# State powers ahead of the third weighed block, and four modulation parts in 32-row strips, in the setup of a two-block transformer kernel

## The chip, the cores and the metric

One core of one Trainium2 chip. The metric is the device time of one execution in microseconds (us), as the median of several runs. Engines: PE is TensorE (matmul), DVE is VectorE, ACT is ScalarE, POOL is GpSimd, SP is SyncE, which here only issues DMAs.

## What is computed

The reference is two transformer blocks, one after the other, in float32 over x of 1024 positions by 1024 channels. The change touches only the start of the first block:

```python
mod = (c @ w_ada + b_ada)[:, None, :]             # c: (1, 1024), w_ada: (1024, 6144)
sh_m, sc_m, gt_m, sh_f, sc_f, gt_f = jnp.split(mod, 6, axis=-1)
h = rms_norm(x, g_pre_mix) * (1.0 + sc_m) + sh_m
z = h @ w_in                                      # (1024, 1280)
u, f, q, k, v = jnp.split(z, splits, axis=-1)
y_ssm = s5_mixer(u, lam_re, lam_im, log_dt, b_re, b_im, c_re, c_im, d_skip, w_glu)
y_fft = fourier_mixer(f, w_fft)
y_att = window_attention(q, k, v, sink)
```

The state-space mixer runs h[t] = lam_bar h[t-1] + b_bar u[t] in both directions for 24 groups of 64 complex states. The kernel does it in chunks of 8 positions, so it needs lam_bar^k b_bar and lam_bar^k c for k up to 8, and lam_bar^(8 * 2^m) to carry states over chunks.

## The kernel before

The order of the work is written out by hand: each engine has one list of instructions, and semaphores join them. All that follows lies in the first 8% of the span.

**The modulation row** c @ w_ada has 12 parts of 512 columns. The first four (0 and 1 are the shift, 2 and 3 the scale) are needed for h. `FIRST_ORDER` is (0, 2, 1, 3). For each, `modulation(j)` on PE (L4239 to L4247) runs eight float32 matmuls. Their stationary operand is a column of c broadcast to 128 columns (`c_bcast`, L3872), so that all 128 rows of a PSUM bank hold the same sums, and `modulation_used(j)` on DVE (L4013 to L4034) picks the diagonal with four multiply-and-reduce instructions against the identity, and adds the bias. The other eight parts are weighed by `weigh_block(b)` on DVE (L4036 to L4052): eight pieces of 128 by 512, each loaded by SP into one of four buffers (`load_block`, L3705), times a column of c, added up in `ada_acc`; `sum_block(b)` on PE sums it over the partitions with four matmuls by a column of ones.

**The loop over x.** ACT squares x (L3777), and DVE and ACT scale half of its rows each (L3863, L3785). In the loop over eight k (L4356 to L4361), PE transposes the columns of x for k + 1 (`turn_input`), ACT applies shift and scale to each half (L3815: one pass for the first half, two for the second), DVE splits off the rounded part (`split_input`, L4116 and L4118), and PE runs `unit_step(0, k)`, six matmuls of unit 0 of h @ w_in. ACT waits for `mod_ready` 1 ahead of the first half (parts 0 and 2) and `mod_ready` 2 ahead of half 8 (parts 1 and 3). Nine more units follow from L4363 on, PE on its own but for `split(n)`: ACT rounds the weights of unit n (L3796) once unit n - 2 is done, and DVE takes the rest (L4109). `sum_block`, `filters` (L4314, 48 matmuls in strips of 32 output rows) and `turn_state` stand in between.

**The state powers.** `lam_step(k)` (L4084 to L4098, six DVE instructions) makes lam_bar^k b_bar for k = 1 to 7. Step 7 releases `lam_b_ready`, for which `filters` waits, and POOL: its `carry_step` chain (L4198) stops there after the first five of its sixteen steps. `square` (L4131 to L4141), nine times, makes the chunk powers `pw`. DVE ends the stage with `weigh_block(7)`, `fold_fourier` (L598 to L602), `late_modulations` (L4054), a wait for `carry_ready` 2 from POOL's last step, and `turns(v, steps, 0)` (L575 to L590), which reads `pw`. Then it copies the transposes of u (L610), for which PE waits at L317; behind them PE runs the chunk transposes, the DFT (14 us) and the attention.

**On DVE**, from the end of the loop over x, the order is: lam 1, split 2, weigh 0, lam 2, split 3, weigh 1, lam 3, split 4, weigh 2, lam 4, split 5, weigh 3, lam 5, split 6, lam 6, the nine squares, lam 7, split 7, weigh 4, first taps, split 8, weigh 5, last taps, weigh 6, split 9, weigh 7.

Of the kernel before, what the change touches and what calls it, by code (L numbers as in the profile page):

```python
# [27 lines left out]
CH = 8  # L28
# [33 lines left out]
def body(ctx, nc, a, out):  # L62
# [49 lines left out]
    junk = place("junk", [P, D], GR + 32 * KB)  # L112
    junk2 = place("junk2", [P, P], RR + 39 * KB + 256)
    c_plain = place("c_plain", [P, 2, PAIRS, GC], RR + 37 * KB)
# [3 lines left out]
    mod_sum = place("mod_sum", [P, 4, KD], RR + 39 * KB)  # L118
    c_bcast = place("c_bcast", [P, KD, P], RR + 40 * KB)
    b_rows = place("b_rows", [4 * PAIRS, P * GC], GR + 40 * KB)  # L120
# [39 lines left out]
    b_turned, lam_used = lam_turned, dt_spread  # L160
    taps_copied, TAPS_0 = dt_spread, 3
    prm_angle, prm_trig, prm_lam = (sem(n) for n in ("prm_angle", "prm_trig", "prm_lam"))
# [3574 lines left out]
    def _(act):  # L3737
# [33 lines left out]


        act.wait_ge(x_in, 16 * NT)
        for n in range(NT):
# [31 lines left out]
        for i in range(2 * KD):  # L3806
            k = i // 2
            act.wait_ge(x_turned, i + 1)
            if i >= 2:
                act.wait_ge(h_ready, i - 1)  # L3810
            if i == KD:
                act.wait_ge(mod_ready, 2)
            half = slice(HALF * (i % 2), HALF * (i % 2 + 1))
            for dst in (h_tmp[i % 2][:], x_hi[:, k, half])[0:1 + i % 2]:
                ins = nc.scalar.activation(dst, bank(6 + i % 2), ACT.Identity, scale=mod_cols[:, 1, k:k + 1], bias=mod_cols[:, 0, k:k + 1])  # L3815
            ins.then_inc(h_made, 1)
            if i == 1:
# [49 lines left out]
    def _(dve):  # L3867
# [3 lines left out]
        dve.wait_ge(small_in, 16)  # L3871
        v.tensor_copy(c_bcast[:], c_cols[:].unsqueeze(2).to_broadcast([P, KD, P])).then_inc(c_spread, 1)  # L3872
        dve.wait_ge(ssm_in, 16 * 4)
# [139 lines left out]
        def modulation_used(j):  # L4013

            dve.wait_ge(ada_mm, FIRST_ORDER.index(j) + 1)
            part, half = j // 2, j % 2
            ps = bank(FIRST_BANKS[j])
            for k in range(4):
                kk = 4 * half + k
                dst = stat_c[:, kk:kk + 1] if part else mod_cols[:, 0, kk:kk + 1]  # L4020

                ins = v.tensor_tensor_reduce(junk2[:], ps[:, P * k:P * (k + 1)], ident[:], 1.0, 0.0, ALU.mult, ALU.add, dst)
                if k < 3:
                    steps.add(ins)
                    steps.settle()
            ins.then_inc(ada_used, 1)
            dve.wait_ge(ada_used, FIRST_ORDER.index(j) + 1)
            cols = slice(4 * half, 4 * half + 4)
            sums = stat_c[:, cols] if part else mod_cols[:, 0, cols]
            steps.add(v.tensor_tensor(sums, sums, bias_cols[:, part, cols], ALU.add))  # L4030
            steps.settle()
            if part:
                steps.add(v.scalar_tensor_tensor(mod_cols[:, 1, cols], sums, 1.0, norm_cols[:, 0, cols], ALU.add, ALU.mult))
                steps.settle()  # L4034
# [138 lines left out]
        weigh_block(4)  # L4173
        first_taps()
        split(8)
# [55 lines left out]
    def _(pe):  # L4231
        t = nc.tensor
        wide = 2 * D_FF // P

        def modulation(j):

            if j == 0:
                pe.wait_ge(ada_half, 16 * KD // 2)
            else:  # L4239
                pe.wait_ge(ada_block[j], 16 * KD)  # L4240
            for k in range(KD):
                if j == 0 and k == KD // 2:
                    pe.wait_ge(ada_block[j], 16 * KD // 2)
                elif j == 3 and k == 5:
                    turn_input(0)
                ins = t.matmul(bank(FIRST_BANKS[j]), c_bcast[:, k, :], ada_w[j][:, k, :], start=(k == 0), stop=(k == KD - 1))
            ins.then_inc(ada_mm, 1)  # L4247
# [15 lines left out]
        def sum_block(b):  # L4263
# [4 lines left out]
            ins.then_inc(ada_mm, 1)  # L4268

        def spread_row(i):  # L4270

# [16 lines left out]
        ins.then_inc(lam_turned, 1)  # L4288
        pe.wait_ge(c_spread, 2)
        modulation(0)  # L4290
        pe.wait_ge(dt_spread, 3)
# [13 lines left out]
        modulation(2)  # L4305
        pe.wait_ge(vec_in, 16 * 8)
# [4 lines left out]
                    ident[0:2 * wide + 4 * KD, 0:2 * wide + 4 * KD]).then_inc(rows_turned, 1)  # L4311
        for j in FIRST_ORDER[2:]:
            modulation(j)

# [37 lines left out]


        pe.wait_ge(ada_used, 2)
        pe.wait_ge(win_lo, 1)
        for k in range(KD):  # L4356
            if k + 1 < KD:
                turn_input(k + 1)
            pe.wait_ge(h_ready, 2 * k + 2)
            ins = unit_step(0, k)  # L4360
        ins.then_inc(win_mm, 1)  # L4361
        for n in range(1, len(win_units)):
# [3 lines left out]
            for k in range(KD):  # L4366
                if 3 <= n <= 6 and k == 1:
                    sum_block(n - 3)
                elif n == 6 and k == 3:
                    filters()  # L4370
                elif n == 6 and k == 7:
                    turn_filters()
                elif n == 7 and k == 4:
                    pe.wait_ge(taps_copied, TAPS_0 + 4)
                    sum_block(4)
                elif n == 8 and k in (1, 6):
                    sum_block(5 + k // 6)
                elif n == 9 and k == 3:
                    sum_block(7)
                if n == 7 and k >= 4:  # L4380
# [58 lines left out]
```

## Time and profile before

| | |
|---|---|
| median of 3 runs | 2896.89 us (2896.32 to 2898.9) |
| the profiled execution's own time | 2893.79 us |
| its span | 2892.0 us |
| PE busy in the span | 2781.0 us (96%) |
| DVE busy | 2066.2 us (71%) |
| ACT busy | 1338.2 us (46%) |
| POOL busy | 247.0 us (9%) |
| granted clock of PE, mean | 0.989 |

The span is the stretch of the trace; 1.8 us of the execution's time lie around it. Times in rows count from the start of the span. A granted clock of 1.00 is 2.4 GHz, 0.50 is 1.2 GHz. A row of a timeline gives start, length, engine and line, and in brackets how long the engine stood idle before it and what released it. Lengths of PE rows are modelled and overlap the next row a little; the difference of two starts is the safer measure.

### The profile page before, as it was taken

Reading aid. Unit: us, or ns where it says so; the run is one execution under the profiler, and the core shown is the slowest. Engines: PE = TensorE matmul, PEld = TensorE weight load, DVE = VectorE, ACT = ScalarE, POOL = GpSimd, SP = SyncE. Lnnn points to the kernel's source line nnn. Section 1 sums busy time; section 2 is a strip of 40 time slices with the busy share of each in tenths; the row PEclk is TensorE's granted clock in tenths of the full one; section 3 lists DMA queues with packets and bytes.
Section 4 is the critical chain, followed back from the end, with each engine's and each line's share of the span. In section 5 each row is a group of like instructions: output and inputs, shape, how many; then the busy total and the mean of one; then the engine's idle time right before and its main releaser. Section 6 shows DMA issues by size and latency. Waiting matters only on the chain.

```text
span 2892.0 us, 37335 instructions
## 1 busy us (share of the span) xinstructions
PE 2781.0 (96%) x13579; PEld 2223.7 (77%) x13579; DVE 2066.2 (71%) x3689; ACT 1338.2 (46%) x2352; POOL 247.0 (9%) x282
## 2 busy tenths in 40 slices
PE   7998899999999999999999999998999999999997
PEld 4874677788888888888888886785677888888886
DVE  6877438989898568766666676897838866665568
ACT  4224746544444554433333453677744433333443
POOL 2063200000000000000000000223610000000000
PEclk9999999999999999999999999999999999999998
DMA  7551043344446773445447763111033355446854
GB/s 236 159 165 23 10 145 124 118 159 155 154 161 230 265 252 120 145 154 168 161 152 281 244 194 110 39 42 34 2 115 111 131 167 164 153 153 211 295 192 145
DMA packets 345429, 436.83 MB, mean 151 GB/s; under 512 B 29701, under 2 KB 191533, under 8 KB 345070
## 3 DMA queue, kind: packets, MB, share of 16 engines
q1 hardware_dynamic: 342290, 428.46, 45.3%
q10 hardware_dynamic: 2956, 5.99, 0.6%
q8 instruction: 108, 1.77, 0.3%
q14 instruction: 75, 0.61, 0.1%
HBM read 317.59 MB, written 116.50 MB: 150 GB/s over the span
## 4 chain that ended last, share of the span: by engine, by line
PE 72%; DVE 7%; ACT 2%; POOL 1%; issue 1%; DMA 0%; DVEq 0%; SPq 0%; ACTq 0%
PE psum L2011 39%; PE psum L1462 21%; PE psum L2974 4%; PE psum L2002 3%; PE psum L1102 2%; DVE count_junk L3505 1%; PE psum L3177 1%; PE psum L3190 1%; PE psum L3164 1%; PE psum L3054 0%; ACT sign_junk L3271 0%; DVE x_t L1708 0%; DVE x_b L2481 0%; POOL p L3672 0%; POOL p_wide L3672 0%
## 5 line engine op out<-in xcount | busy, mean ns | idle before, releaser
L1462 PE MATMUL psum<-far_op,far_op 128*128 128x512 f32 x2772 | 629.4, 389 | 0.0
L1462 PEld LDWEIGHTS psum<-far_op,far_op 128*128 128x128 f32 x2772 | 520.1, 188 | 108.0
L2011 PE MATMUL psum<-x_b,w_near 128*128 128x512 f32 x1440 | 346.0, 389 | 0.8 <-DVE w_near L1634 0.8
L2011 PE MATMUL psum<-x_t,w_near 128*128 128x512 f32 x1440 | 336.5, 389 | 1.7 <-ACT psum L1748 1.7
L2011 PE MATMUL psum<-x_t,w_far 128*128 128x512 f32 x1440 | 336.3, 389 | 0.0
L2011 PEld LDWEIGHTS psum<-x_t,w_near 128*128 128x128 f32 x1440 | 270.2, 188 | 58.2 <-ACT psum L1748 2.1
L2011 PEld LDWEIGHTS psum<-x_b,w_near 128*128 128x128 f32 x1440 | 270.2, 188 | 57.3 <-issue 1.2
L2011 PEld LDWEIGHTS psum<-x_t,w_far 128*128 128x128 f32 x1440 | 270.2, 188 | 56.3 <-ACT u_keep L1760 0.2
L1226 ACT CAST far_op<-far_a 128x512 fp32r<-128x512 f32 x231 | 143.9, 623 | 315.9 <-PE psum L1462 305.4
L1233 DVE TENSOR_TENSOR far_op<-far_a,far_op 128x512 fp32r<-128x512 f32 x231 | 159.8, 692 | 176.4 <-ACT far_op L1226 175.1
L2011 PE MATMUL psum<-x_b,w_far 128*128 128x512 f32 x720 | 173.1, 389 | 1.7 <-DVE val_row L1880 1.7
L3640 POOL TENSOR_TENSOR split_lo<-raw,split_hi 128x256 fp32r<-128x256 f32 (+1 forms) x60 | 44.8, 781 | 1458.3 <-ACT split_hi L2990 1458.3
L1235 DVE TENSOR_TENSOR far_op<-far_b,far_op 128x512 fp32r<-128x512 f32 x231 | 159.2, 689 | 0.0
L1634 DVE TENSOR_TENSOR w_far<-w_sum,w_far 128x512 fp32r<-128x512 f32 x120 | 82.4, 686 | 106.4 <-ACT w_far L1628 106.4
L2011 PEld LDWEIGHTS psum<-x_b,w_far 128*128 128x128 f32 x720 | 135.1, 188 | 30.1 <-DVE val_row L1880 2.1
L1227 ACT CAST far_op<-far_b 128x512 fp32r<-128x512 f32 x231 | 142.1, 615 | 0.0
L1628 ACT CAST w_far<-w_sum 128x512 fp32r<-128x512 f32 x120 | 73.9, 616 | 119.0 <-PE psum L2011 119.0
L1634 DVE TENSOR_TENSOR w_near<-w_sum,w_near 128x512 fp32r<-128x512 f32 x120 | 80.9, 688 | 64.1 <-ACT w_near L1628 64.0
L1628 ACT CAST w_near<-raw 128x512 fp32r<-128x512 f32 (+1 forms) x129 | 82.8, 642 | 72.3 <-PE psum L2011 61.3
L1634 DVE TENSOR_TENSOR w_far<-raw,w_far 128x512 fp32r<-128x512 f32 (+1 forms) x66 | 47.2, 715 | 88.6 <-ACT w_far L1628 88.6
L1079 DVE TENSOR_TENSOR src_lo<-yc_t,src_hi 128x512 fp32r<-128x512 f32 x31 | 21.4, 692 | 119.0 <-ACT w_out_hi L1072 119.0
L2002 PE MATMUL psum<-x_b,w_near 128*128 128x512 f32 x360 | 90.8, 400 | 8.5 <-DVE x_b L2319 4.1
(531 smaller groups left out, 4769.7 us busy)
## 6 DMA issues: line engine op xcount, KB each, us to landing
far_a<-row_ops SPq DMA_DIRECT2D x231, 256.0 KB, 3.0
row_ops<-hidden SPq DMA_DIRECT2D x99, 512.0 KB, 5.6
raw<-in_ffn_w SPq DMA_DIRECT2D x88, 512.0 KB, 4.7
col_sums<-hidden SPq DMA_DIRECT2D x66, 512.0 KB, 5.7
far_b<-col_sums SPq DMA_DIRECT2D x132, 256.0 KB, 3.5
raw<-in_w_up SPq DMA_DIRECT2D x44, 512.0 KB, 3.9
hidden<-in_ffn_w SPq DMA_DIRECT2D x44, 512.0 KB, 5.2
far_b<-in_ffn_w SPq DMA_DIRECT2D x66, 256.0 KB, 3.6
```

The costliest lines, as they stand in the source:

```text
L1102: ins = t.matmul(bank(2 * n + c), l[:, P * n:P * (n + 1)], r[:, HALF * c:HALF * (c + 1)], start=(first and m == 0), stop=(last and m == 2))
L1226: s.copy(far_a_hi[slot][:], far_a[late][t % FB][:]).then_inc(f_hi, 1)
L1227: s.copy(far_b_hi[slot][:], far_b[late][t % FB][:]).then_inc(f_hi, 1)
L1233: v.tensor_tensor(far_a_lo[slot][:], far_a[late][t % FB][:], far_a_hi[slot][:], ALU.subtract).then_inc(f_lo, 1)
L1235: v.tensor_tensor(far_b_lo[slot][:], far_b[late][t % FB][:], far_b_hi[slot][:], ALU.subtract).then_inc(f_lo, 1)
L1462: ins = t.matmul(bank(b + n), l[slot][:, rows], r[slot][:], start=(fresh and i == 0 and m == 0), stop=(i == FH - 1 and m == 2), skip_group ...
L1628: nc.scalar.copy(op_parts(p, i)[0], op_source(p, i)).then_inc(op_hi, 1)
L1634: nc.vector.tensor_tensor(lower, op_source(p, i), upper, ALU.subtract).then_inc(op_lo, 1)
L2002: ins = t.matmul(bank(b), at[:, l, cols], r, start=(first and m == 0), stop=(last and m == 2))
L2011: ins = t.matmul(bank(b), at[:, l, cols], x[:, k, r], start=(start and k == 0 and m == 0), stop=(k == 3 and m == 2), skip_group_check=not ...
L2974: ins = t.matmul(bank(2 * slot + half)[0:m], l[:, P * k:P * k + m], r[:, k, HALF * half:HALF * (half + 1)], start=(k == 0 and i == 0), sto ...
L3640: ins = g.tensor_tensor(tile_of(w_rest, m)[:, k:k + 2], tile_of(raw[slot], m)[:, k:k + 2], tile_of(w_top, m)[:, k:k + 2], ALU.subtract)
```

## The change

`c_bcast` becomes `c_strip`, 32 columns for each k, and each of the first four parts is made in two steps: `strips(j)`, eight matmuls of which number k writes the 32 rows of strip k % 4 of the bank, and `strip_sums(j)`, four matmuls that take a copy of the bank as the stationary operand and a column with a one in each strip (`sel_cols`) as the moving one, so that the part comes out as columns. ACT makes the copy (`copy_strips`). `modulation_used` is left with the bias and the scale. Parts 1 and 3 move into the loop over x. On DVE the powers 3 to 7 are made in a row before the third weighed block, and the squares go behind the last one.

```diff
+        def copy_strips(j):
+            at = FIRST_ORDER.index(j)
+            act.wait_ge(strips_done, STRIPS_0 + at + 1)
+            act.wait_ge(dt_spread, 3)
+            if at:
+                act.wait_ge(ada_mm, at)
+            nc.scalar.copy(ada_part[:], bank(FIRST_BANKS[j])).then_inc(mod_copied, 1)
+
+        copy_strips(0)
         act.wait_ge(x_in, 16 * NT)
...
         nc.scalar.activation(stat_b[:, 0:NT], stat_a[:, NT:2 * NT], ACT.Sqrt).then_inc(x_std, 1)
+        copy_strips(2)
...
             if i == 1:
                 split(1)
+            elif i in (3, 5):
+                copy_strips(i - 2)
...
-            if n == 7:
+            if n == 6:
                 act.wait_ge(k_mm, 1)
...
-            for k in range(4):
-                kk = 4 * half + k
-                dst = stat_c[:, kk:kk + 1] if part else mod_cols[:, 0, kk:kk + 1]
-                ins = v.tensor_tensor_reduce(junk2[:], ps[:, P * k:P * (k + 1)], ident[:], 1.0, 0.0, ALU.mult, ALU.add, dst)
...
-            steps.add(v.tensor_tensor(sums, sums, bias_cols[:, part, cols], ALU.add))
+            steps.add(v.tensor_tensor(sums, bank(FIRST_BANKS[j], 4), bias_cols[:, part, cols], ALU.add))
...
             split_input(i)
-            if i == 2:
+            if i == 4:
+                split(1)
+            elif i == 5:
                 modulation_used(1)
-            elif i == 4:
+            elif i == 7:
                 modulation_used(3)
                 dve.sem_inc(mod_ready, 1)
-            elif i == 7:
-                split(1)
...
         lam_step(1)
-        for b in range(4):
-            split(2 + b)
-            weigh_block(b)
-            lam_step(2 + b)
+        split(2)
+        weigh_block(0)
+        lam_step(2)
+        split(3)
+        weigh_block(1)
+        lam_step(3)
+        lam_step(4)
+        split(4)
+        for k in range(5, CH):
+            lam_step(k)
+        split(5)
+        weigh_block(2)
         split(6)
-        lam_step(CH - 2)
-        square(pw[:, 0, 1], pw[:, 1, 1], col(12), col(10))
-        for src, dst in ((1, 2), (2, 0)) + tuple((m, m + 1) for m in range(6)):
-            square(pw[:, 0, dst], pw[:, 1, dst], pw[:, 0, src], pw[:, 1, src], pw[:, :, src])
-        lam_step(CH - 1)
+        weigh_block(3)
+        first_taps()
         split(7)
         weigh_block(4)
-        first_taps()
...
         dve.sem_inc(fw_zero, 1)
+        square(pw[:, 0, 1], pw[:, 1, 1], col(12), col(10))
+        for src, dst in ((1, 2), (2, 0)) + tuple((m, m + 1) for m in range(6)):
+            square(pw[:, 0, dst], pw[:, 1, dst], pw[:, 0, src], pw[:, 1, src], pw[:, :, src])
         fold_fourier(dve, v, steps)
...
+                s = k % 4
+                ins = t.matmul(bank(FIRST_BANKS[j])[32 * s:32 * (s + 1)], c_strip[:, k, :], ada_w[j][:, k, :], start=(k < 4), stop=(k >= 4))
+            ins.then_inc(strips_done, 1)
+
+        def strip_sums(j):
+            pe.wait_ge(mod_copied, COPIED_0 + FIRST_ORDER.index(j) + 1)
+            for i in range(4):
+                ins = t.matmul(bank(FIRST_BANKS[j], 1, i), ada_part[:, P * i:P * (i + 1)], sel_cols[:], start=True, stop=True)
             ins.then_inc(ada_mm, 1)
...
+        SUMS_AT = ((3, 1), (4, 1), (6, 1), (7, 1), (7, 6), (8, 2), (8, 7), (9, 4))
...
+        turn_input(0)
         pe.wait_ge(ada_used, 2)
         pe.wait_ge(win_lo, 1)
         for k in range(KD):
             if k + 1 < KD:
                 turn_input(k + 1)
+            if k in (1, 2):
+                strips(2 * k - 1)
+            if k in (2, 3):
+                strip_sums(2 * k - 3)
             pe.wait_ge(h_ready, 2 * k + 2)
             ins = unit_step(0, k)
```

On PE, `strips(0)` with its sums stands behind the transposes of b and c, and `strips(2)` with its sums behind those of the vectors; `modulation(1)` and `modulation(3)`, which stood between them and the first transposes of x, are gone. `filters` moves from step (6, 3) of the units to (5, 2), `turn_filters` from (6, 7) to (5, 6), and `sum_block(b)` goes by `SUMS_AT`: before, it stood at k = 1 of units 3 to 6, then at (7, 4), (8, 1), (8, 6) and (9, 3).

## Rows read from the trace of the kernel before

**Rows 1.** The page, first line.
```profile
span 2892.0 us, 37335 instructions
```

**Rows 2.** Windows: stretch, length, busy us of PE, PEld, DVE, ACT, POOL, PEclk, DMA share, GB/s.
```profile
24.00:26.00 2.00, 0.00 (x0) 0.00 (x0) 1.85 (x6) 0.00 (x0) 0.00 (x0) 0.50 1.04 402
...
34.00:36.00 2.00, 2.00 (x4) 0.87 (x3) 1.97 (x5) 1.94 (x5) 1.82 (x4) 0.50 1.05 385
...
38.00:40.00 2.00, 2.00 (x6) 0.80 (x6) 0.00 (x0) 1.97 (x3) 1.92 (x5) 1.00 0.96 355
...
78.30:151.20 72.90, 72.90 (x424) 60.85 (x423) 60.88 (x115) 13.48 (x16) 10.96 (x13) 1.00 0.60 176
...
151.20:192.76 41.56, 41.56 (x226) 35.16 (x224) 29.82 (x39) 11.89 (x17) 40.30 (x52) 1.00 0.55 163
```

**Rows 3.** Timeline of PE, setup: start us, us, engine, line, what [idle before <-releaser].
```profile
31.38 10.05 PE L4246 MATMUL psum<-ada_w,c_bcast 128*128 128x512 f32 x16 [8.67 <-DMA ada_w<-in_w_ada]
...
41.47 11.33 PE L4246 MATMUL psum<-ada_w,c_bcast 128*128 128x512 f32 x26
...
56.88 0.71 PE L4349 MATMUL psum<-x_hi,win_upper 128*128 128x512 f32 x2
...
60.88 0.73 PE L4349 MATMUL psum<-x_hi,win_upper 128*128 128x512 f32 x2 [1.33 <-DVE x_lo L4118]
...
69.45 0.73 PE L4349 MATMUL psum<-x_hi,win_upper 128*128 128x512 f32 x2
...
76.81 0.73 PE L4349 MATMUL psum<-x_hi,win_upper 128*128 128x512 f32 x2 [0.68 <-DVE x_lo L4118]
```

**Rows 4.** Timeline of ACT, setup.
```profile
49.41 1.03 ACT L3796 CAST win_upper<-win_raw 128x1024 fp32r<-128x1024 f32 x1
...
53.34 1.45 ACT L3815 ACTIVATE h_tmp<-psum,mod_cols 128x512 f32<-128x512 f32 x2 [2.90 <-PE psum L4260]
```

**Rows 5.** Timeline of DVE, setup.
```profile
45.29 2.74 DVE L3863 TENSOR_SCALAR x_rows<-x_rows,stat_b 128x1024 f32<-128x1024 f32 x4
...
51.38 1.22 DVE L4109 TENSOR_TENSOR win_lower<-win_raw,win_upper 128x1024 fp32r<-128x1024 f32 x1 [0.22 <-DVE mod_cols L4033]
...
54.61 0.69 DVE L4118 TENSOR_TENSOR x_lo<-h_tmp,x_hi 128x512 fp32r<-128x512 f32 x1
```

**Rows 6.** Timeline of PE and ACT: the nearest rows for the new operations.
```profile
140.69 2.83 PE L4322 MATMUL psum<-lam_b,c_pad 128*32 128x128 f32 x96
...
156.50 0.94 PE L4267 MATMUL psum<-one_cols,ada_acc 128*128 128x1 f32 x8
...
157.98 0.59 ACT L3790 COPY state_in<-psum 128x512 f32<-128x512 f32 x1 [4.76 <-PE psum L4341]
```

**Rows 7.** Lines of DVE from 80 to 140, then 140 to 182: busy us, mean ns.
```profile
L4049 DVE SCALAR_TENSOR_TENSOR ada_acc<-ada_piece,c_cols,ada_acc 128x512 f32<-128x512 f32 x28 | 21.0, 751 | 7.3 <-DMA ada_piece<-in_w_ada 5.2
...
L4049 DVE SCALAR_TENSOR_TENSOR ada_acc<-ada_piece,c_cols,ada_acc 128x512 f32<-128x512 f32 x28 | 24.0, 855 | 6.9 <-DMA ada_piece<-in_w_ada 4.8
```

**Rows 8.** Timeline of DVE, later.
```profile
131.62 0.18 DVE L4134 TENSOR_TENSOR prm<-prm 128x24 f32<-128x24 f32 x1
...
136.69 0.56 DVE L4090 TENSOR_TENSOR w_tmp<-lam_b,prm 128x384 f32<-128x384 f32 x1
...
152.35 1.22 DVE L4109 TENSOR_TENSOR win_lower<-win_raw,win_upper 128x1024 fp32r<-128x1024 f32 x1 [0.28 <-ACT win_upper L3796]
...
180.85 1.11 DVE L4049 SCALAR_TENSOR_TENSOR ada_acc<-ada_piece,c_cols,ada_acc 128x512 f32<-128x512 f32 x1 [0.49 <-DMA ada_piece<-in_w_ada]
...
182.61 0.95 DVE L598 TENSOR_TENSOR f_diff<-f_t 128x511 f32<-128x511 f32 x1
...
194.23 0.07 DVE L575 MEMSET turn<- 128x12 f32 x1 [5.50 <-POOLq L4227]
```

**Rows 9.** Timeline of POOL, then of PE.
```profile
139.93 1.53 POOL L4208 TENSOR_TENSOR e_tmp<-carry_out,prm 128x192 f32<-128x192 f32 x1 [95.42 <-DVEq L4097]
...
208.32 3.53 PE L317 MATMUL psum<-ident,u_t 128*128 128x128 f32 x16 [5.69 <-DVE u_rows L610]
```

More of the change, by code:

```diff
@@ L112, in body @@
     junk = place("junk", [P, D], GR + 32 * KB)
-    junk2 = place("junk2", [P, P], RR + 39 * KB + 256)
+    sel_cols = place("sel_cols", [P, 1], RR + 39 * KB + 256)
+    ada_part = place("ada_part", [P, HALF], RR + 40 * KB)
     c_plain = place("c_plain", [P, 2, PAIRS, GC], RR + 37 * KB)
@@ L118, in body @@
     mod_sum = place("mod_sum", [P, 4, KD], RR + 39 * KB)
-    c_bcast = place("c_bcast", [P, KD, P], RR + 40 * KB)
+    c_strip = place("c_strip", [P, KD, P // 4], RR + 43 * KB)
     b_rows = place("b_rows", [4 * PAIRS, P * GC], GR + 40 * KB)
@@ L160, in body @@
     b_turned, lam_used = lam_turned, dt_spread
-    taps_copied, TAPS_0 = dt_spread, 3
+    mod_copied, COPIED_0, strips_done, STRIPS_0 = dt_spread, 3, c_turned, 2
+    taps_copied, TAPS_0 = dt_spread, 7
     prm_angle, prm_trig, prm_lam = (sem(n) for n in ("prm_angle", "prm_trig", "prm_lam"))
@@ L3871, in _ @@
         dve.wait_ge(small_in, 16)
-        v.tensor_copy(c_bcast[:], c_cols[:].unsqueeze(2).to_broadcast([P, KD, P])).then_inc(c_spread, 1)
+        steps.add(v.memset(sel_cols[:], 0.0))
+        steps.settle()
+        for s in range(4):
+            steps.add(v.memset(sel_cols[32 * s:32 * s + 1], 1.0))
+        steps.add(v.tensor_copy(c_strip[:], c_cols[:].unsqueeze(2).to_broadcast([P, KD, P // 4])))
+        steps.settle()
+        dve.sem_inc(c_spread, 1)
         dve.wait_ge(ssm_in, 16 * 4)
@@ L4015, in modulation_used @@
             dve.wait_ge(ada_mm, FIRST_ORDER.index(j) + 1)
-            part, half = j // 2, j % 2
-            ps = bank(FIRST_BANKS[j])
-            for k in range(4):
-                kk = 4 * half + k
-                dst = stat_c[:, kk:kk + 1] if part else mod_cols[:, 0, kk:kk + 1]
-                ins = v.tensor_tensor_reduce(junk2[:], ps[:, P * k:P * (k + 1)], ident[:], 1.0, 0.0, ALU.mult, ALU.add, dst)
[L4023 to L4028, printed above, removed]
+            part, cols = j // 2, slice(4 * (j % 2), 4 * (j % 2) + 4)
             sums = stat_c[:, cols] if part else mod_cols[:, 0, cols]
-            steps.add(v.tensor_tensor(sums, sums, bias_cols[:, part, cols], ALU.add))
+            steps.add(v.tensor_tensor(sums, bank(FIRST_BANKS[j], 4), bias_cols[:, part, cols], ALU.add))
             steps.settle()
+            dve.sem_inc(ada_used, 1)
             if part:
@@ L4233, in _, with strips @@
         wide = 2 * D_FF // P
[L4235 to L4240, printed above, removed]
+        def strips(j):
+            pe.wait_ge(ada_half if j == 0 else ada_block[j], 16 * KD // (2 if j == 0 else 1))
             for k in range(KD):
@@ L4243, in modulation @@
                     pe.wait_ge(ada_block[j], 16 * KD // 2)
-                elif j == 3 and k == 5:
-                    turn_input(0)
-                ins = t.matmul(bank(FIRST_BANKS[j]), c_bcast[:, k, :], ada_w[j][:, k, :], start=(k == 0), stop=(k == KD - 1))
+                s = k % 4
[5 more added lines that the diff above has]
+                ins = t.matmul(bank(FIRST_BANKS[j], 1, i), ada_part[:, P * i:P * (i + 1)], sel_cols[:], start=True, stop=True)
             ins.then_inc(ada_mm, 1)
@@ L4288, in _ @@
         ins.then_inc(lam_turned, 1)
-        pe.wait_ge(c_spread, 2)
-        modulation(0)
         pe.wait_ge(dt_spread, 3)
@@ L4304, in _ @@
             ins.then_inc(c_turned, 1)
-        modulation(2)
+        pe.wait_ge(c_spread, 2)
+        strips(0)
+        strip_sums(0)
         pe.wait_ge(vec_in, 16 * 8)
@@ L4311, in _ @@
                     ident[0:2 * wide + 4 * KD, 0:2 * wide + 4 * KD]).then_inc(rows_turned, 1)
-        for j in FIRST_ORDER[2:]:
-            modulation(j)
+        strips(2)
+        strip_sums(2)
         def filters():
@@ L4366, in _ @@
             for k in range(KD):
-                if 3 <= n <= 6 and k == 1:
-                    sum_block(n - 3)
-                elif n == 6 and k == 3:
+                if (n, k) == (5, 2):
                     filters()
-                elif n == 6 and k == 7:
+                elif (n, k) == (5, 6):
                     turn_filters()
[L4373 to L4379, printed above, removed]
+                elif (n, k) in SUMS_AT:
+                    if (n, k) == SUMS_AT[2]:
+                        pe.wait_ge(taps_copied, TAPS_0 + 4)
+                    sum_block(SUMS_AT.index((n, k)))
                 if n == 7 and k >= 4:
```

## The prediction

> **What bounds the kernel now.** I read the page first, then the windows and timelines of the first 210 us, since the change touches nothing later. The span is 2892.0 us [rows 1], so what is at stake is 8% of it. The windows show one long stretch in which PE never stops: 72.90 of 72.90 us from 78.30 to 151.20, 41.56 of 41.56 from there to 192.76 [rows 2]. Those are units 1 to 9 with their sums, filters and transposes. Here DVE, ACT and POOL cost nothing as long as they are in time, and the stretch moves with the end of unit 0. Two places are not bound so. Ahead of it, the first matmul of unit 0 starts at 56.88 and unit 0 ends at 78.30, that is 21.4 us for what the even steps 4 to 7, 2.45 us each (69.45 to 76.81), would do in 19.6; PE idles, 1.33 us ahead of step 1 alone [rows 3]. Behind it, PE stands idle 5.69 us until 208.32 for the copies of u [rows 9], which wait on DVE behind `turns`, and `turns` stood idle 5.50 us until 194.23 for POOL's last step [rows 8]. So the time is set by three pieces: the start of the loop, the loop, and DVE's tail behind the last weighed block.
>
> **Start of the loop.** Before, PE was in parts 2, 1 and 3 nearly all the time from 31.38 to the loop (10.05 us for the first of them, at a clock of 0.50 in part, then 26 instructions in 11.33) [rows 2, 3]. Each part becomes strips. The nearest row is `filters`: 96 instructions of 128 columns in strips of 32 rows in 2.83 us, 29.5 ns each [rows 6], where the full-width rows give 11.33 / 26 = 436 ns for 512 columns [rows 3], or 109 for 128: the strips run nearly four at a time. So 16 instructions take 16 x 436 x 29.5 / 109 = 1.9 us instead of 7.0, at full clock. From both sides: 7.0 if they don't overlap at 512 columns, 1.75 if they overlap fully. I take 1.9, for `filters` has the same order of strips in one bank. The sums are like `sum_block`, 0.94 of which 0.8 is its own; the copy is 0.59, like that of `state_in` [rows 6].
> DVE has its x rows scaled at 45.29 + 2.74 = 48.0. The two parts cost it 3.3 us until 51.38 [rows 5]; now three small instructions, some 0.7. What is late next is ACT, which ends scaling at 49.41 and rounds unit 0's weights until 50.44 [rows 4]. So `split(0)` on DVE starts at 50.5, not 51.38, and ACT's first half at 50.5, not 53.34, where it had waited 2.90 for PE's transposes [rows 4]. After 1.22 for the split and 1.1 + 0.6 for the halves (cast 0.43 and a subtraction of 0.69 [rows 5]) both halves are there at 53.4. **Unit 0 starts at 53.5, 3.4 us earlier.** Strips 0 and 2, their sums, and copies on ACT stand in PE's and ACT's waits for DMA and cost nothing; if that cover were gone, strips 2, its sums and copy would cost 2 x (1.9 + 0.8) + 0.6 = 6 at half clock. The transposes of b and c come ahead of strips 0 and let DVE go earlier, which ends in the same wait for ACT. SP's first unit loads go out earlier, as the vector columns do, behind all w_ada and x transfers; nothing waits for them.
>
> **The loop.** PE gets 2 x (1.9 + 0.8) = 5.4 us into it, the copies stand in ACT's chain, and ACT now waits for the strips with the next halves queued behind it. Also PE has done little since 36. The windows show 0.50 (1.2 GHz) from 24 to 26, with PE idle, still 0.50 from 34 to 36, three us into full work, and 1.00 from 38 [rows 2]. I take half clock until about 58. In order: step 0 at half clock 53.5 to 56.2; transposes for step 2 to 58.0; strips 1 to 59.9; step 1 (1.4 each) to 61.3. ACT, held at its copy until 60.1, does it and two halves (0.6 + 0.7 + 1.4), so the transposes for step 3 end at 63.3; strips 3 to 65.2, sums 1 to 66.0, step 2 to 67.4; ACT again copy and two halves, transposes to 68.6, sums 3 to 69.4, step 3 to 70.8. Half 8 waits for DVE's scale (70.2), halves 8 and 9 end at 72.3, and step 4 starts at 73.1 where it stood at 69.45. From there as before, 7.4 to step 7 and 1.5 for it [rows 3]: 82.0. **Unit 0 ends 3.7 us later** than at 78.30. Bounds: with no idle left on PE it would be 53.5 + 21.4 - 4 + 5.4 = 76.3, 2 earlier; with half clock until 62, 2 more, 84.
> The Trainium skill (TensorE: Matmul & The Clock Gate, What's actually happening) calls the slow clock the default that only activity lifts, a rule that speaks against taking work off PE ahead of this loop. By it the loop ends at 82.0 as above; without it, at full clock throughout, at 80.0, and the sum below would be 2.0 less.
>
> **DVE's order.** lam 3 to 7 ahead of the third block and the squares out of the middle change nothing by themselves: PE is full there, and what DVE loses or gains it waits for at `split(8)`, where it stood idle 0.28 for ACT [rows 8] behind unit 6. The new order is in time everywhere by my count: split 4 done at about 114 for unit 4 at 115.6, lam 7 at 122 for filters at 130, split 6 near 134 (its load is now issued only in the third block) for unit 6 at 142. One sum (0.8) moves from ahead of unit 6's end to behind it, so `split(8)` comes 3.7 - 0.8 later. POOL's eleven steps run from 139.93 to 194, 54 us; now from about 122 to 176. Beside POOL a weighing instruction takes 855 ns, without it 751 [rows 7]: the last eight and their split save 0.5 of 0.8, as part waits for DMA. The last block ends at 181.96 [rows 8], now + 3.7 - 0.8 - 0.5 = 184.4.
> **The tail.** Before, from 181.96 to 194.23, 12.3 us, of them 5.50 idle [rows 8]. Now the wait is gone, the squares (131.62 to 136.69, 5.1 [rows 8]) are in, and the fold is off POOL: its instruction took 0.95 [rows 8] where one on 512 elements without POOL takes 0.69 [rows 5]; six save 1.5. 12.3 - 5.5 + 5.1 - 1.5 = 10.4: 1.9 less. The powers' early finish thus buys a wait of 5.5 and the squares cost 5.1 of it. PE's own path to the copies (idle from 202.6) moves to 206.3, and DVE's to 208.3 + 3.7 - 0.8 - 0.5 - 1.9 = 208.8, so DVE still ends last. Behind it all goes on as before: PE's DFT covers DVE's second `turns`.
> **Sum:** -3.4 at the start, +7.1 in the loop, -0.8, -0.5, -1.9: +0.5 us. Against the profiled execution's own 2893.79 that is 2894.3; the median of the runs is 3.1 above it, so 2897.4. I call 0.2% (5.8 us) about what a measurement can tell from no change.
>
> **The rivals.**
> A: the new work hides in PE's idle time. For it: PE idled some 4 us in the loop. Then unit 0 ends at 76.3, 5.7 before my forecast: -5.2, 2891.7; the start of a shift past 5.8. Against it: ACT's copies stand in the chain of the halves. A warm clock alone gives 2895.4. Chance 0.14.
> B, the other side, and also that the change doesn't do what it says: the strips don't overlap at 512 columns. Strips 1 and 3 then take 7.0 each, + 10.2 in the loop: 2907.6. It decides from 4.6 us a part on (1.9 and half of the 5.3 that lack to 5.8). Against it: `filters`. Chance 0.07.
> C: DVE's tail gives nothing: the last blocks are paced by their DMAs (waits of 6.9 in the second row of [rows 7]), the fold is no faster, and the late load of unit 6 holds PE for 2. + 0.5 + 1.5 + 2: 2901.4. Chance 0.12.
>
> **How the numbers follow.** Forecast 0.67, all but 0.03 of it within 0.2%. A gives half to faster (0.07), B slower, C 0.05 slower. With 0.02 for shifts that I don't see: faster 0.10, within 0.77, slower 0.13. The range takes in A at 2891.7 and C at 2901.4 with a little more: 2891.5 to 2902.
>
> **What would show it.** Right: L4246's 64 instructions gone, strips of 16 in about 1.9 us at full clock; unit 0's first matmul near 53.5, unit 1's near 82 (78.31 before); a clock of 0.50 after 40; PE then full until 196; POOL's last step near 176; no wait for POOL ahead of `turns`, whose start stands near 195; PE's idle before L317 shorter, 2.5 us. Wrong: unit 1 starting before 79 or after 85, strips of over 4.6 us, a PE wait for `win_lo` or for a sum in units 1 to 9, or a first copy of u that doesn't follow DVE.

## The result, and the profile after

The kernel after took 2907.31 us in the median of 9 runs (2897.88 to 2913.75), the kernel before beside it 2897.81 (2894.82 to 2907.27): a ratio of 1.0025, interval 1.0013 to 1.0037. Three repeats gave 1.0011, 1.0022 and 1.0024 (below); the mean of the four is 1.0020, or 5.9 us slower. The forecast was +0.5 us, 2897.4, in a range up to 2902.0: the time is outside it. Slower by more than 0.2%, as the first ratio has it, had a chance of 0.13.

The profiled execution took 2901.27 us, its span 2899.5 at a mean granted clock of 0.985, where the one before took 2893.79 at 0.989. First the page of after, the span and the clock over 40 slices:

```profile
span 2899.5 us, 37382 instructions
...
PEclk8998999999999999999999999999999999999999
```

The first slice fell from 9 to 8: half clock that goes with the new idle time of PE ahead of the loop over x. (The fourth, behind the setup, reads 8 too.) PE's timeline ahead of and in the loop, which answers to [rows 3]:

```profile
51.54 1.94 PE L4279 MATMUL psum<-ident,x_rows 128*128 128x128 f32 x8 [1.20 <-DVE win_lower L4118]
53.16 1.22 PE L4370 MATMUL psum<-x_hi,win_upper 128*128 128x512 f32 x2
...
56.84 1.92 PE L4258 MATMUL psum<-ada_w,c_strip 128*32 128x512 f32 x16
...
62.08 1.92 PE L4258 MATMUL psum<-ada_w,c_strip 128*32 128x512 f32 x16
63.93 1.05 PE L4265 MATMUL psum<-sel_cols,ada_part 128*128 128x1 f32 x8
...
80.08 0.73 PE L4370 MATMUL psum<-x_hi,win_upper 128*128 128x512 f32 x2 [0.61 <-DVE x_lo L4127]
...
81.55 0.62 PE L4370 MATMUL psum<-x_hi,win_upper 128*128 128x512 f32 x2
```

Unit 0 starts at 53.16, the strips take 1.92 us for 16 instructions, unit 1 starts at 81.55. The first matmuls of unit 0 still run at half clock (1.22 us where a pair at full clock has 0.72). Two windows show it, 0.64 and 0.51 of full speed where the kernel before had 0.94 and 1.00 in the same windows (both kernels' rows, after first):

```profile
36.00:46.00 10.00, 1.71 (x8) 1.72 (x8) 2.93 (x16) 9.15 (x17) 6.61 (x13) 0.64 1.11 347
46.00:56.00 10.00, 6.85 (x25) 5.24 (x26) 6.76 (x13) 9.06 (x12) 0.00 (x0) 0.51 0.36 106
56.00:60.00 4.00, 4.00 (x31) 2.13 (x29) 0.00 (x0) 1.17 (x3) 0.00 (x0) 1.00 0.00 0
```
```profile
36.00:46.00 10.00, 10.00 (x25) 4.45 (x24) 4.18 (x18) 8.68 (x15) 8.12 (x16) 0.94 0.66 228
46.00:56.00 10.00, 10.00 (x30) 4.77 (x29) 7.67 (x27) 7.10 (x9) 0.00 (x0) 1.00 0.68 220
```

ACT in the loop, to set beside [rows 4]: it stands idle ahead of its two copies for 3.77 and 3.66 us.

```profile
58.83 0.59 ACT L3781 COPY ada_part<-psum 128x512 f32<-128x512 f32 x1 [3.77 <-PE psum L4258]
...
65.09 0.59 ACT L3781 COPY ada_part<-psum 128x512 f32<-128x512 f32 x1 [3.66 <-PE psum L4265]
```

DVE later, to set beside [rows 8]: the turns no longer wait for POOL, but three splits now wait for ACT, 2.52, 0.82 and 1.86 us, where before one waited 0.28.

```profile
132.19 1.23 DVE L4118 TENSOR_TENSOR win_lower<-win_raw,win_upper 128x1024 fp32r<-128x1024 f32 x1 [2.52 <-ACT win_upper L3808]
143.88 1.57 DVE L4118 TENSOR_TENSOR win_lower<-win_raw,win_upper 128x1024 fp32r<-128x1024 f32 x1 [0.82 <-ACT win_upper L3808]
155.53 1.23 DVE L4118 TENSOR_TENSOR win_lower<-win_raw,win_upper 128x1024 fp32r<-128x1024 f32 x1 [1.86 <-ACT win_upper L3808]
...
189.46 0.69 DVE L600 TENSOR_TENSOR f_diff<-f_t 128x511 f32<-128x511 f32 x1
...
194.06 0.07 DVE L577 MEMSET turn<- 128x12 f32 x1
```

The end of POOL's chain, and PE's wait for the copies of u, which answer to [rows 9]:

```profile
177.10 1.05 POOL L4230 TENSOR_TENSOR carry_out<-e_tmp 128x192 f32<-128x192 f32 x1
```
```profile
208.16 1.31 PE L319 MATMUL psum<-ident,u_t 128*128 128x128 f32 x8 [2.23 <-DVE u_rows L612]
```

By this row the setup ends 0.16 us earlier than before (208.32). The span is 7.5 us longer all the same. Matching instruction by instruction (time after minus time before of the same instruction of DVE), the shift is +2 from 500 to 2000 us and +7.5 from 2240 on. One pair of profiles is thus no ground for a verdict, and the experiments give more of them.

### The profile page after: what moved, and what is told of

It is laid out like the page before. It is cut to its first block, busy times and chain, and to the rows that moved or that the text cites. A ratio compares the mean times of both kernels' runs of the same rounds, so it can differ in the third digit from the quotient of the medians.

```text
span 2899.5 us, 37382 instructions
## 1 busy us (share of the span) xinstructions
PE 2775.0 (96%) x13611; PEld 2222.5 (77%) x13611; DVE 2063.5 (71%) x3662; ACT 1340.4 (46%) x2356; POOL 250.6 (9%) x282
## 4 chain that ended last, share of the span: by engine, by line
PE 71%; DVE 8%; ACT 2%; issue 1%; POOL 1%; DMA 0%; DVEq 0%; SPq 0%; ACTq 0%
PE psum L2013 39%; PE psum L1464 21%; PE psum L2004 3%; PE psum L2976 3%; PE psum L1104 2%; DVE count_junk L3507 2%; PE psum L3179 1%; PE psum L3166 1%; PE psum L3192 1%; PE psum L3056 0%; ACT sign_junk L3273 0%; DVE x_t L1710 0%; POOL p_wide L3674 0%; PE psum L2644 0%; DVE x_lo L2556 0%
## 5 line engine op out<-in xcount | busy, mean ns | idle before, releaser
L1081 DVE TENSOR_TENSOR src_lo<-yc_t,src_hi 128x512 fp32r<-128x512 f32 x31 | 21.4, 692 | 119.0 <-ACT w_out_hi L1074 118.9
```

## The experiments

Four marks are read from every trace: U0, the first matmul of unit 0; U1, the first of unit 1; T, the start of `turns` on DVE; X, the second group of chunk transposes (L317 or L319), for which PE waits. One table for all, in us, in order of time; ratios are to the kernel before on the same chip, with their intervals.

| kernel | U0 | U1 | T - U1 | X | ratio |
|---|---|---|---|---|---|
| before (on record) | 56.88 | 78.31 | 115.9 | 208.32 | |
| after (on record) | 53.16 | 81.55 | 112.5 | 208.16 | 1.0025 (1.0013 to 1.0037) |
| e1 after again | 53.30 | 82.59 | 114.3 | 211.01 | 1.0011 (1.0002 to 1.0020) |
| e2 strips only | 52.58 | 81.00 | 115.1 | 210.17 | 1.0030 (1.0018 to 1.0043) |
| e3 order only | 55.82 | 77.23 | 112.7 | 204.04 | 0.9987 (0.9976 to 0.9998) |
| e4 warm | 52.84 | 81.35 | 115.5 | 210.93 | 1.0016 (1.0006 to 1.0026) |
| e5 unit loads | 53.03 | 82.30 | 111.5 | 207.85 | 1.0011 (1.0001 to 1.0021) |
| e6 parts ahead | 52.70 | 75.22 | 114.2 | 203.46 | 1.0006 (0.9997 to 1.0015) |
| e7 both | 52.95 | 75.03 | 111.7 | 200.81 | 0.9985 (0.9974 to 0.9995) |
| e8 before again | 55.17 | 76.61 | 115.8 | 206.44 | 1.0000 (0.9991 to 1.0008) |
| e9 order and loads | 55.89 | 77.31 | 110.3 | 202.10 | 0.9978 (0.9967 to 0.9989) |
| e10 filled | 52.89 | 80.14 | 115.5 | 209.75 | 1.0009 (0.9998 to 1.0020) |
| e11 both again | 52.38 | 73.38 | 113.8 | 201.24 | 0.9979 (0.9967 to 0.9991) |
| e12 after, third | 53.20 | 81.72 | 113.1 | 208.91 | 1.0022 (1.0010 to 1.0034) |
| e13 delay | 55.21 | 76.64 | 121.9 | 212.59 | 1.0014 (1.0004 to 1.0024) |
| e14 before, third | 55.19 | 76.64 | 114.8 | 205.54 | 0.9997 (0.9986 to 1.0008) |
| e15 after, fourth | 52.93 | 81.07 | 113.8 | 208.98 | 1.0024 (1.0012 to 1.0036) |
| e16 e9 again | 55.59 | 77.03 | 110.1 | 201.82 | 0.9978 (0.9967 to 0.9989) |

**Which half of the change costs (e1 to e4).**

> The changed kernel once more, to see a second execution of it. In its first profile DVE's copies of u start at 207.41, 0.16 before the kernel before, and the 7.5 us of the span come later. Theory L (the loop over x and PE's clock): that profile was a lucky one, its clock rose at 55.8; another shows unit 1 starting later than 81.6, up to 85, and the time is 6 to 10 above the kernel before. Theory N (nothing in the setup; the loss lies behind it, in the attention and the second block, where stretches of half clock come and go): unit 1 again near 81.6, the copies of u near 207.4, and the time 5 to 10 above.

Unit 1 is later than in the first profile, at 82.59, on the side of theory L, but the time is 3.2 us above the kernel before and not 5 to 10: neither theory has it.

e2 is the kernel after with DVE's order, `filters` and the sums back where they were:

```diff
...
-        for k in range(5, CH):
-            lam_step(k)
-        split(5)
-        weigh_block(2)
+        for b in range(4):
+            split(2 + b)
+            weigh_block(b)
+            lam_step(2 + b)
...
```

> Strips alone, DVE's order, the filters and the sums as before. Theory L: unit 1 starts at 81.6 or later; DVE's tail has no gain from the order (turns wait for POOL, which is released 3 us later): 3 to 6 us slower than before by the tail alone, and as slow as the changed kernel or slower, +6 to +12. Theory N: the same, only that the copies of u start 3 us later and the rest is noise, +3. Theory O (the new order on DVE costs the time): 0 to +1.

e3 is the reverse, the kernel before with the new order (powers in a row, squares behind the last block, `SUMS_AT`) and its four parts at full width.

> DVE's new order, the filters and sums at their new places, the modulation as before. Theory L: unit 0 as before (unit 1 at 78.3), the tail 3.2 us shorter: 3 us faster than before. Theory O: +6 to +8. Theory N: 3 us earlier at the copies of u, -3, or whatever the later clock makes of it.

The two halves have opposite signs, as theory L has it. The order alone gains 0.13% (3.8 us), the strips alone cost 0.30% (8.7 us), together -3.8 + 8.7 = +4.9 against the 5.9 measured. The strips' cost stands at U1, 81.0 to 82.6 in every kernel with strips in the loop and no fillers that hold the clock. It is not all there: e2 has X at 210.17, 3.6 us behind the mean of the kernel before (206.6, below), and its ratio says 8.7 (5.2 to 12.5). e4 meant to keep the clock up:

```diff
         strips(2)
+        for _ in range(9):
+            t.matmul(bank(0), ident[:], ada_w[2][:, 0, :], start=True, stop=True)
         strip_sums(2)
+        for _ in range(1):
+            t.matmul(bank(0), ident[:], ada_w[2][:, 0, :], start=True, stop=True)
```

> The changed kernel with ten matmuls more on PE, of 128x512 into a bank that is overwritten later, between strips 2 and the first transposes of x; they only keep PE at work. Theory L: the clock is 1.00 when the loop starts, unit 1 starts at 80 instead of 81.6 or later, and the time is 2 to 5 us less than that of the changed kernel, with less spread. Theories N and O: no difference to the changed kernel beyond 1.6 us.

It missed its aim: the windows show the clock at 1.00 from 36 to 44 but at half again from 46 to 54, so it decides nothing on the clock. U1 and the ratio (81.35, 1.0016) are those of the kernel after.

**The unit loads (e5).** Why do three splits wait? In the kernel after, SP's timeline (SPq is its queue) shows the load of unit 6 (its two DMAs at 125.64) behind the pieces of block 2, whose issue took 24.57 us; before, it went out at 108.19.

```profile
99.92 1.06 SPq L3704 DMA_DIRECT2D win_raw<-in_w_in  x2
101.02 24.57 SPq L3720 DMA_DIRECT2D ada_piece<-in_w_ada  x8
125.64 1.18 SPq L3704 DMA_DIRECT2D win_raw<-in_w_in  x2
```

SP issues in the order of its list, and a piece's load waits there until DVE has used the piece four before it. The new order puts the powers 4 to 7, which came behind block 2, on DVE ahead of it, so the pieces, and all behind them, stand still. e5 moves one call:

```diff
                 sp.dma_start(ada_piece[n % 4][:], w_ada[:, k, cols]).then_inc(piece_in[n % 4], 16)
+                if k == 3 and b + 4 < len(win_units):
+                    load_unit(b + 4)
...
             load_block(b)
-            if b + 4 < len(win_units):
-                load_unit(b + 4)
```

> The kernel after, with one move on SP: the load of the weights of unit b + 4 is issued behind the fourth piece of block b, no longer behind the eighth. In the kernel after, the eighth piece is issued only when DVE has used the fourth, so the load of unit 6 goes out at 125.6 us, after 24.6 us for the pieces of block 2, and DVE then stands idle 2.52, 0.82 and 1.86 us ahead of split(6), (7) and (8) for ACT, which waits for the load. Theory S (these 5.2 us are a cost of the new order that the prediction left out): the three waits shrink to under 1 us together, the turns on DVE start 3 to 5 us earlier against unit 1 than in the kernel after (112.5 us after the first step of unit 1 there, 108 to 110 here), and the time falls by 3 to 5 us to 2899 to 2900 where the kernel after has 2903.4. Rival (PE sets the path up to split(8), so DVE only waits elsewhere): the idle time moves to the later splits or to the pieces, the turns start within 1 us of where they did, and the ratio to the kernel before stays at 1.001 to 1.0025.

The splits of e5, same view as above:

```profile
131.83 1.31 DVE L4118 TENSOR_TENSOR win_lower<-win_raw,win_upper 128x1024 fp32r<-128x1024 f32 x1
144.16 1.39 DVE L4118 TENSOR_TENSOR win_lower<-win_raw,win_upper 128x1024 fp32r<-128x1024 f32 x1
155.41 1.23 DVE L4118 TENSOR_TENSOR win_lower<-win_raw,win_upper 128x1024 fp32r<-128x1024 f32 x1 [2.13 <-ACT win_upper L3808]
```

Two of the three waits are gone, and T - U1 is 111.5 where the four traces of the kernel after have 112.5 to 114.3, 113.4 in the mean: 1.9 us, less than the 3 to 5 of theory S. The ratio, 1.0011, lies where the rival had it and does not tell this gain from nothing. The third wait is as long as before but has another cause. In the kernel after, ACT rounds unit 8's weights when their DMA lands; in e5, as in the kernel before, when PE has ended unit 6. Here is that instruction in e1, in e5 and in the kernel before:

```profile
157.78 1.06 ACT L3808 CAST win_upper<-win_raw 128x1024 fp32r<-128x1024 f32 x1 [10.72 <-DMA win_raw<-in_w_in]
```
```profile
154.32 1.05 ACT L3808 CAST win_upper<-win_raw 128x1024 fp32r<-128x1024 f32 x1 [9.88 <-PE psum L4370]
```
```profile
151.26 1.05 ACT L3796 CAST win_upper<-win_raw 128x1024 fp32r<-128x1024 f32 x1 [0.52 <-PE psum L4349]
```

So it is in all 18 traces: for units 6, 7 and 8 the releaser is the DMA in the eight with the new order and the old place of the loads, PE in the ten others. Counted from U1, `split(8)` starts at 74.05 in the kernel before (mean of four), at 73.7 to 76.5 in those eight (74.95 in the mean of the kernel after), and at 73.1 in e5, e7, e9 and e16. The 1.9 us of e5 stand there.

**Parts ahead of the loop (e6, e7, e11).** Three copies go to DVE, as `copy_part`, and the strips to PE's idle time ahead of the loop:

```diff
-        copy_strips(2)
...
-            elif i in (3, 5):
-                copy_strips(i - 2)
...
+        copy_part(2)
         x_norm(dve, v, steps)
+        copy_part(1)
...
+            if i == 1:
+                copy_part(3)
...
         strip_sums(2)
+        strips(1)
+        strips(3)
...
         turn_input(0)
+        strip_sums(1)
...
-            if k in (1, 2):
-                strips(2 * k - 1)
-            if k in (2, 3):
-                strip_sums(2 * k - 3)
+            if k == 1:
+                strip_sums(3)
```

> The kernel after, with the strips of parts 1 and 3 ahead of the loop over x, as in the kernel before, and the copies of parts 2, 1 and 3 on DVE, so that nothing new stands in PE's and ACT's lists inside the loop but the sums of part 3. Theory L (the loop's loss of 3.2 us comes from strips, sums and copies inside it and from the half clock): unit 0 starts at 53 as in the kernel after, unit 1 at 75 to 77 where it started at 81.6 (78.3 before), a shift of -5 to -6; the whole kernel follows by -3 to -6, 2897 to 2900 in the median, if DVE's waits at the splits don't eat it. Rival (the chain of halves through ACT and DVE and the half clock set the loop's time whatever stands beside it): unit 1 starts at 79 or later. Rival 2 (unit 1 starts early but the splits wait for their loads instead): unit 1 at 76, split(8) not over 2 us earlier than the 155.5 of the kernel after.

U1 is at 75.22, 6.5 us earlier than in the kernel after (81.73 in the mean of four), as theory L has it. The waits at the splits are still there and eat part of it (this is e6):

```profile
126.11 1.23 DVE L4123 TENSOR_TENSOR win_lower<-win_raw,win_upper 128x1024 fp32r<-128x1024 f32 x1 [2.57 <-ACT win_upper L3807]
138.35 1.23 DVE L4123 TENSOR_TENSOR win_lower<-win_raw,win_upper 128x1024 fp32r<-128x1024 f32 x1 [0.82 <-ACT win_upper L3807]
151.62 1.23 DVE L4123 TENSOR_TENSOR win_lower<-win_raw,win_upper 128x1024 fp32r<-128x1024 f32 x1 [3.07 <-ACT win_upper L3807]
```

At X, e6 is 3.1 us ahead of the kernel before, but its ratio of 1.0006 (-0.9 to +4.3 us) does not show that lead: here too the median is slower than the setup says.

> Both moves together: parts 1 and 3 ahead of the loop, and the loads of the units behind the fourth piece. If theories S and L hold and add up, the turns on DVE start 7 to 10 us earlier than in the kernel after (194.1), the chunk transposes too unless PE then waits for something else, and the time is 2893 to 2896 in the median, 0.997 to 0.999 of the kernel before. If only one of the two sets the path, it is as fast as the better of e5 and e6, within 1.5 us.

> e7 once more, unchanged. From unit 1 to the turns 111.7 again and unit 1 at 75 within 1 us. Theory T (stretches at half clock behind 210 us are drawn anew in every run): the second profile differs from the first by 2 to 6 us between 300 and 2300 us. Ratio 0.998 to 0.999. Rival (e7 falls always into the long half-clock stretch of 13.7 us near 330 us): that stretch is there again, at the same place in the program.

Both moves add up at X, which comes at 200.8 and 201.2, 8.2 us earlier than the 209.3 of the kernel after, with ratios of 0.9985 and 0.9979. What e11 should have repeated it did not: unit 1 is at 73.38 and T - U1 at 113.8, where e7 has 75.03 and 111.7.

**The best kernel (e9, e16), the kernel before with the new order and e5's loads.**

> The kernel before with the new order of DVE (as e3) and with the unit loads behind the fourth piece (as e5): the first four parts stay full-width and ahead of the loop. Theory S2 (the unit loads are worth 1 to 3 us from unit 1 to the turns, whatever stands ahead): from unit 1 to the turns 111.0 to 112 us, where e3 took 112.7 and the kernel before 115.9; unit 1 at 77 to 78; time 0.9975 to 0.9985 of the kernel before. Rival (the unit loads are worth nothing, as the ratio of e5 says, 1.0011 as e1's): the same ratio as e3, 0.9987, and 112.7 us.

> The kernel of e9 (new order of DVE, unit loads behind the fourth piece, parts at full width ahead of the loop) once more. If its gain holds: from unit 1 to the turns 110 to 111.5 us where the kernel before takes 115.8, ratio 0.9970 to 0.9985. If e9 was a lucky draw: 0.9985 to 0.9995, as e3.

As expected: 0.9978 twice, 6.4 us faster than the kernel before and 12 than the one after, without strips for the first four parts. T - U1 is 110.3 and 110.1, 2.4 and 2.6 below the one trace of e3: of that 1.0 stands at `split(8)`, the rest in the weighing behind it. The ratios alone, 0.9978 and 0.9987, would not tell e9 from e3. e7 starts unit 1 earlier by 2.3 us than e9 and reaches X 1.3 us earlier, and its ratios are no better. More of its lead goes into PE's wait for DVE ahead of X, first e9, then e7:

```profile
202.10 1.31 PE L317 MATMUL psum<-ident,u_t 128*128 128x128 f32 x8 [0.41 <-DVE u_rows L610]
```
```profile
200.81 1.31 PE L319 MATMUL psum<-ident,u_t 128*128 128x128 f32 x8 [1.40 <-DVE u_rows L612]
```

**The clock in the loop (e10),** the kernel after with 11 fillers of e4's kind between strips 2 and their sums, 2 behind them, 1 behind the first transposes of x.

> The kernel after with 14 matmuls whose results nobody uses in PE's idle time ahead of the loop: 11 between strips(2) and its sums, 2 behind them, 1 behind the first transposes of x (e4 had 9, 1 and 0, and its clock fell again at 45.5 us). The outputs are unchanged. Theory K (the half clock is 2 us of the loop's loss): the windows from 46 to 56 us show a clock of 1.00 for the most part, unit 0 starts at 53, unit 1 at 79.3 to 80.3 instead of 81.6 to 82.6. Rival (the loop is bound by the copies in ACT's chain and the half clock is hidden behind them): unit 1 still at 81.3 or later with a full clock. If the clock is half again from 46 on, it tells nothing between the two, but says that more than this is needed to keep it.

This time the clock holds:

```profile
36.00:46.00 10.00, 10.00 (x30) 4.79 (x30) 2.69 (x11) 9.15 (x16) 6.03 (x12) 0.98 1.07 339
46.00:56.00 10.00, 8.21 (x45) 4.82 (x48) 6.49 (x13) 8.79 (x11) 0.00 (x0) 1.00 0.32 103
```

From U0 to U1 it takes 27.3 us, the four traces of the kernel after 28.1 to 29.3, 28.6 in the mean, the kernel before 21.4. By this one trace the half clock is 1.3 of the 7.2 us by which the loop grew; the prediction had 2.0. The rest goes when strips and copies leave the loop (e6: 22.5). At X nothing of the 1.3 is left, 209.75 against 209.3: `split(8)` is among the late ones here, 76.4 from U1.

**What lies behind the setup (e8, e12 to e15).**

> The kernel before, unchanged, for a second profile and for the spread. Theory T (the stretches at half clock behind 210 us come and go with the run and cost 1 to 5 us each): the setup repeats to within 1 us (unit 1 at 78.3, turns at 194.2), the second profile's instructions behind 1780 us stand 2 to 6 us later against those at 500 us than in the first, as they did in the four profiles of changed kernels, and the ratio is 1.000 within 0.001. Rival (the stretches are set off by what the change did to the setup): the second profile repeats the first within 1 us up to the end.

The same program came out 7.2 us longer than on record, as theory T has it; but the setup moved by more than the 1 us that it allowed, 1.7 at unit 1 and 1.9 at X. Windows from 2000 to 2260, in the second block, first e8, then the kernel before on record:

```profile
2000.00:2260.00 260.00, 238.96 (x1666) 176.57 (x1663) 167.74 (x334) 149.28 (x290) 82.81 (x76) 0.97 0.23 76
```
```profile
2000.00:2260.00 260.00, 237.52 (x1680) 177.85 (x1677) 171.70 (x336) 151.12 (x287) 81.65 (x74) 0.99 0.23 78
```

> The kernel after once more, for a third profile of it against the two of the kernel before (e8 and the one on record). If the change costs what the setup says, 2 to 3 us: turns at 193 to 197, ratio 1.0005 to 1.0015. Rival (the change costs more behind the setup, by way of the clock): ratio over 1.002, and the third profile again over 5 us longer behind 500 us than the second one of the kernel before (e8).

The ratio is the rival's, 1.0022, but not by what the rival says: matched by instructions, this trace stands 4.5 us behind the one on record of before at 2300 us, e8's 7.2.

> The kernel before with 30 copies of one column block into another that nobody reads any more (128x24, one behind the other, 0.21 us each by the steps of the squares), on DVE between its wait for POOL and the turns: a delay of 6.3 us for the turns, the copies of u and PE's chunk transposes, and nothing else changed. Theory U (a shift of the setup is worth itself and no more in the median): 6.3 us, a ratio of 1.0022, 1.0012 to 1.0032. Rival V (a later start behind idle time costs more by the clock, as the kernel after seems to): over 9 us, 1.0032 or more. Rival W (DVE's path is not what PE waits for): under 3 us.

The delay came out as built: 30 copies in 6.34 us, and PE's wait grew to 11.64.

```profile
192.06 6.34 DVE L4188 COPY prm<-prm 128x24 f32<-128x24 f32 x30 [6.00 <-POOLq L4230]
```
```profile
212.59 1.76 PE L317 MATMUL psum<-ident,u_t 128*128 128x128 f32 x7 [11.64 <-DVE u_rows L610]
```

The median rose by 1.0014, 4.1 us (1.2 to 7.0). That holds theory U's 6.3 and leaves out V's 9: a later setup costs itself, not more. W's 3 lies in the interval too; against it stands the trace, where T and X moved by 5.8 against the other three of that kernel.

> The kernel before, unchanged: its third profile. The chunk transposes of PE at 206.4 to 208.3 as in the two others, unit 1 at 76.6 to 78.3; the end 3 to 8 us later than in the profile on record; ratio 1.000 within 0.001.

> The kernel after, unchanged: its fourth profile, beside e14 on the same chip. If only the setup counts: transposes at 208 to 211, ratio 1.0003 to 1.0015. If something behind it counts too: ratio 1.0015 to 1.003 again.

Now the setup can be compared over several traces. For the kernel before there are four (e13 counts, its 6.34 us taken off), for the one after four: X at 206.6 (205.5 to 208.3) against 209.3 (208.2 to 211.0). **The setup ends 2.6 us later by the traces, and the ratios say 5.9.** Each ratio is known to 0.0009 to 0.0012, so the mean of four to about 0.0006, 4.2 to 7.6 us. The four traces of the kernel after come from executions of 2894.8 to 2904.0 us, while its medians are 2903 to 2907; the slower ones left no trace here. What the other 3.3 us are stays open. That a delay multiplies is excluded by e13. The clock behind the setup carries a part at most. The mean granted clock is on record for every execution: 0.9832 over the 45 of the kernel after, 0.9865 over 160 of the kernel before. As clock lost (the missing share times the span) that is 48.8 us against 39.1, and up to X the four traces of each lose 14.6 and 7.1 in the mean. So some 2 us more are lost behind X. From one execution of a kernel to the next, a us of clock lost goes with 0.5 us of time; by that, as an estimate, they are 1 of the 3.3 us. The setup's own spread and chance were not told apart.

## Why the prediction was wrong

**Start of the loop.** Predicted U0 at 53.5; it came at 52.9 to 53.3. Right as a time. As a difference it is 2.5 us, not 3.4: the trace on record had U0 at 56.88, the three others of that program 55.2.

**The loop.** Strips of 1.9 us: 1.92, right, and rival B falls. Unit 1 at 82.0: 81.1 to 82.6, right, with the waits of ACT where they were put. Against the kernel before it is +4.7, predicted +3.7, for the same reason as above. Rival A, hiding in PE's idle time, failed: 7.4 us of ACT's waits stand in the chain of the halves. e6 shows that its place made the work dear: the same strips ahead of the loop, with the copies on DVE, give 75.2.

**DVE's order.** This is the step that failed by its mechanism: "The new order is in time everywhere by my count: ... split 6 near 134 (its load is now issued only in the third block)". The late load was seen, and its price was set at nothing because PE needed unit 6 only at 142. PE indeed never waited for these weights. But units 7 and 8 are loaded late as well, and DVE, whose list ends last, stands idle for each. The sentence "what DVE loses or gains it waits for at `split(8)`" rests on PE's unit 6 releasing that split; in the kernel after the DMA of unit 8 does. So the term of -0.8 ("`split(8)` comes 3.7 - 0.8 later") came out as +0.9, 74.95 from U1 instead of 74.05. With the loads moved it is 73.1 (e5, e7, e9, e16), -0.9, as forecast: the sum on PE was priced right, and the late loads, priced at nothing, cost 1.8. The other two terms were -0.5 for the weighing, measured -1.3, and -1.9 for the tail, measured -1.7. Together -3.2 was forecast, and four traces of either kernel give 113.4 - 115.5 = -2.1.

**The tail.** Right but for 0.2: POOL ends at 178 (predicted 176), no wait for it, fold instructions of 0.69 instead of 0.95, turns at 194.1 to 196.9 (predicted 195).

**The sum and the median.** +0.5 became +2.6 at X. Of the 2.1 us missing, 1.0 is the loop against a trace of before that was late there, 1.1 the order. The time itself was missed by 9.9. Of these, 2.1 are those two terms; 3.3 are what the ratios say above the traces (5.9 - 2.6) and stay open; 3.6 are the first comparison, whose medians of nine runs each lie 9.5 apart where four ratios say 5.9; 0.9 is the kernel before, 2897.81 there and 2896.89 in the runs shown. So besides the -0.8, the step from the setup to the median failed, and by more (the last three, 7.8 of the 9.9): "the median of the runs is 3.1 above it". It carried the distance of the kernel before, 2896.89 - 2893.79, over to the kernel after, whose median lay 6.0 above its profiled execution (2907.31 - 2901.27), as if the difference of two medians were known as well as the sum. Why that part is as large stays open. The range had bounds for terms of the setup alone, 5.9 down and 4.6 up, and none for this. Rival C, on the right side, had the late load of unit 6, but as holding PE, which never waited for it; that its 2901.4 is nearer than the forecast is luck.

## What to carry to other kernels

Where two streams of loads share one issuing queue, a load inherits the waits of those ahead of it: reordering the consumer of one stream moves the arrival of the other. Put the load that is needed on the path ahead of the piece whose buffer is not free yet. Work taken into idle time of an engine must not stand in the list of another engine that feeds the path (here ACT's copies); the same strips some 18 us earlier, with the copies on another engine, were worth 6.5 us at the end of the first unit. And a change worth 0.1% can't be read from one pair of profiles of a kernel whose repeated traces differ by 0.3%.

## What the runs showed that was not expected

The granted clock differs from one execution of the same program to the next, in the same stretch of it. From 330 to 350 us, where PE is idle a sixth of the time, e8 shows 0.91 and e14, the same program, 0.66:

```profile
330.00:350.00 20.00, 16.64 (x171) 12.78 (x165) 0.36 (x2) 12.00 (x40) 2.39 (x3) 0.91 0.00 1
```
```profile
330.00:350.00 20.00, 18.34 (x150) 14.17 (x151) 0.36 (x2) 8.57 (x27) 0.04 (x1) 0.66 0.00 1
```

By matching instructions, e14 takes 3.7 us more there than e8; 8 of the 18 traces have it: e7 and e11 both, as the rival to theory T had it, but also e14 and e13, and e16 where the same program as e9 has not. The stretch from 2000 to 2260 us, in the second block, takes 3 to 9.5 us more than on record in 10 of the 18 traces and at most 0.7 more in the other 8, again with no pattern by kernel. The Trainium skill (TensorE: Matmul & The Clock Gate, What's actually happening) says that the number of slow matmuls is variable from run to run of one kernel; the trace agrees. It puts the penalty of the ramp at under 1% of a typical span and advises not to fit a specific count. What comes and goes between two traces of the kernel before is 7 us of 2899, under 1% too, but it is more than the change.

In e4 PE was filled from 34.8 to 43.0 and again from 44.0 to 46.3, with 0.98 us idle between, and the windows show the clock at half again from 46 to 54. With four more fillers (e10) it held at 1.00 to 60.
